# Expert weights of a mixture-of-experts layer loaded and multiplied in blocks of 1024 columns instead of 512

## What is computed

```python
def swiglu(x, w13, w2):
    gate, up = jnp.split(x @ w13, 2, axis=-1)
    return (jax.nn.silu(gate) * up) @ w2

def moe_swiglu(x, router, w13, w2):
    ...
    for e in range(N_EXPERTS):
        out = out + gates[..., e:e + 1].astype(x.dtype) * swiglu(x, w13[e], w2[e])
    return out
```

## Time and profile before

| | |
|---|---|
| median of 3 runs | 1877.17 us (1876.15 to 1878.55) |
| the profiled execution | 1874.99 us, its span 1873.2 us |
| matmuls busy (PE) | 1777.7 us, 95% |
| VectorE busy | 1303.8 us, 70% |
| ScalarE busy | 979.8 us, 52% |
| HBM read | 464.36 MB, 248 GB/s over the span |

### The profile page before, as it was taken

One profiled execution on the slowest core, in us unless ns is written; L12 is line 12 of the kernel. 1 busy time (PEld: TensorE's weight loads), 2 busy tenths in 40 slices (PEclk: granted clock), 3 DMA queues, 4 the chain that ended last, 5 costly groups with the idle time before them and its releaser, 6 DMA issues.

```text
span 1873.2 us, 21553 instructions
## 1 busy us (share of the span) xinstructions
PE 1777.7 (95%) x7962; PEld 1390.5 (74%) x7962; DVE 1303.8 (70%) x1217; ACT 979.8 (52%) x861; POOL 13.8 (1%) x22
## 2 busy tenths in 40 slices
PE   7999998999989998888999999999999999999996
PEld 6846674788867465747788888888888888888885
DVE  5464544445454554445988989889899898898996
ACT  4333122344233331314767767777677777776773
POOL 0000000000000000000000000000000000000000
PEclk9998799999999988997999999999999999999998
DMA  8523052454545231346999999999999999999991
GB/s 288 180 90 112 22 181 90 164 184 170 178 160 180 90 112 61 120 143 233 349 366 347 367 342 364 369 347 361 345 360 371 344 360 359 355 364 342 365 359 63
DMA packets 206471, 466.19 MB, mean 249 GB/s; under 512 B 11952, under 2 KB 14416, under 8 KB 206416
## 3 DMA queue, kind: packets, MB, share of 16 engines
q1 hardware_dynamic: 200880, 463.76, 68.9%
q10 hardware_dynamic: 5536, 1.68, 0.4%
HBM read 464.36 MB, written 1.05 MB: 248 GB/s over the span
## 4 chain that ended last, share of the span: by engine, by line
PE 90%; DVE 6%; ACT 2%; issue 1%; DMA 1%; POOL 0%; ACTq 0%; DVEq 0%; SPq 0%
PE ps L1427 22%; PE ps L1823 16%; PE ps L1825 16%; PE ps L1824 16%; PE ps L1454 6%; PE ps L1745 3%; PE ps L1803 2%; PE ps L1812 1%; PE ps L1618 1%; DVE w_lo L871 1%; PE ps L1388 1%; PE ps L1671 1%; PE ps L1653 1%; PE ps L1537 1%; PE ps L1580 1%
## 5 line engine op out<-in xcount | busy, mean ns | idle before, releaser
L871 DVE TENSOR_TENSOR w_lo<-ring,w_hi 128x2048 fp32r<-128x2048 f32 x336 | 767.7, 2289 | 120.5 <-ACT w_hi L556 117.5
L556 ACT CAST w_hi<-ring 128x2048 fp32r<-128x2048 f32 x336 | 641.9, 1911 | 280.1 <-PE ps L1825 265.1
L1823 PE MATMUL ps<-w_hi,xe_hi 128*128 128x512 f32 x896 | 353.2, 394 | 3.2 <-DVE w_lo L871 1.8
L1825 PE MATMUL ps<-w_hi,xe_lo 128*128 128x512 f32 x896 | 349.3, 390 | 0.0
L1824 PE MATMUL ps<-w_lo,xe_hi 128*128 128x512 f32 x896 | 348.7, 389 | 0.0
L1823 PEld LDWEIGHTS ps<-w_hi,xe_hi 128*128 128x128 f32 x896 | 168.2, 188 | 38.7 <-DVE w_lo L871 2.7
L1825 PEld LDWEIGHTS ps<-w_hi,xe_lo 128*128 128x128 f32 x896 | 168.1, 188 | 35.8
L1824 PEld LDWEIGHTS ps<-w_lo,xe_hi 128*128 128x128 f32 x896 | 168.4, 188 | 33.8
L1823 PE MATMUL ps<-w_hi,he_hi 128*128 128x512 f32 x448 | 178.2, 398 | 0.0
L1825 PE MATMUL ps<-w_hi,he_lo 128*128 128x512 f32 x448 | 174.8, 390 | 0.0
L1824 PE MATMUL ps<-w_lo,he_hi 128*128 128x512 f32 x448 | 174.4, 389 | 0.0
(11 more groups left out here) (260 smaller groups left out, 1846.1 us busy)
## 6 DMA issues: line engine op xcount, KB each, us to landing
ring<-in_moe_w_dram SPq DMA_DIRECT2D x336, 1024.0 KB, 5.5
ring<-in_ffd_w_dram SPq DMA_DIRECT2D x31, 1024.0 KB, 5.0
ring<-in_w_in_dram SPq DMA_DIRECT2D x24, 1024.0 KB, 5.5
ring<-in_xa_wkv_dram SPq DMA_DIRECT2D x16, 1024.0 KB, 5.0
ring<-in_w_out_dram SPq DMA_DIRECT2D x8, 1024.0 KB, 5.0
ring<-in_xa_wq_dram SPq DMA_DIRECT2D x8, 1024.0 KB, 4.9
ring<-in_xa_wo_dram SPq DMA_DIRECT2D x8, 1024.0 KB, 5.1
ring<-in_ffd_w_dram SPq DMA_DIRECT2D x4, 512.0 KB, 3.6
```

The lines of the kernel that those rows point to most:

```text
L556: act.copy(w_hi[:, q % SPLIT_SLOTS, :], ring[:, q % RAW_SLOTS, :]).then_inc(hi_ready, 1)
L871: dve.tensor_tensor(w_lo[:, q % SPLIT_SLOTS, :], ring[:, q % RAW_SLOTS, :], w_hi[:, q % SPLIT_SLOTS, :].bitcast(F32), ALU.subtract).then_i ...
L1823: pe.matmul(ps[:, bank, :], x_hi, hi[:, c, cols], start=first, stop=False)
L1825: return pe.matmul(ps[:, bank, :], x_lo, hi[:, c, cols], start=False, stop=last)
```

## The change

Gate and up are taken in blocks of 1024 columns: three wide blocks m = 0, 1, 2 and one of 512 columns (m = 3). A half of a wide block is 2 chunks of 128 rows times 1024 columns (still 1 MB, runs of 4 KB), and a wide block has four halves of gate (q = 8m to 8m + 3), then four of up (8m + 4 to 8m + 7). The last block keeps halves of 4 chunks times 512 columns, two of gate (24, 25), two of up (26, 27). Gate uses banks 0 and 1, up banks 2 and 3, for every block. The silu reads two banks in one operation, behind high(6), (14), (22) and, one bank, (28). The hge operations come in pairs behind low(10), (18), (26), and one behind (30). The transposes stand behind halves 11, 13, 19, 21, 27, 29, 31, and he_hi and he_lo four halves later. TensorE waits for the silu before each gate block and for the hge before each up block. In a wide half each row chunk is multiplied into one bank and then the other, three matmuls each. Nothing else moves; the scatter is that of the kernel before.

```diff
--- before.py
+++ after.py
@@ -75,10 +75,27 @@
 HIGH_SLOTS = 4
 MOE_PAIRS = F_MOE // N
 ITEM_HALVES = 6 * MOE_PAIRS
+WIDE = F_MOE // (2 * N)
+BLOCKS = WIDE + 1
+
+
+def moe_half(q):
+
+    if q < 8 * WIDE:
+        return q // 4 % 2, 2 * (q % 4), 2, q // 8 * 2 * N, 2 * N
+    r = q - 8 * WIDE
+    return r // 2, 4 * (r % 2), 4, WIDE * 2 * N, N
+
+
+GATE_DONE = [8 * m + 4 for m in range(WIDE)] + [4 * MOE_PAIRS - 2]
+UP_DONE = [8 * m + 8 for m in range(WIDE)] + [4 * MOE_PAIRS]
+SILU_AT = [q + 2 for q in GATE_DONE]
+HIDDEN_AT = [q + 2 for q in UP_DONE]
 UNITS = 7
 
 
-TURNED_AT = [4 * n + 11 for n in range(MOE_PAIRS - 1)] + [35]
+TURN_AT = [11, 13, 19, 21, 27, 29, 31]
+TURNED_AT = [q + 4 for q in TURN_AT]
 GATHERED_AT = [37, 40]
 SCATTERED_AT = [4, 5, 10, 11]
 ADDED_AT = [7, 8, 13, 14]
@@ -365,7 +382,7 @@
 
         def half_view(buffer, q, slots):
 
-            return buffer[:, q % slots, :].rearrange("p (c n) -> p c n", c=4 if q < 4 * MOE_PAIRS else 2)
+            return buffer[:, q % slots, :].rearrange("p (c n) -> p c n", c=moe_half(q)[2] if q < 4 * MOE_PAIRS else 2)
 
         def piece_bank(i):
 
@@ -436,9 +453,9 @@
             def item_half(q, i, e):
 
                 if q < 4 * MOE_PAIRS:
-                    c0 = (q // 2 % 2) * F_MOE + q // 4 * N
-                    r = 4 * (q % 2)
-                    src = a["moe_w13"][0, e].rearrange("(c p) n -> p c n", p=P)[:, r:r + 4, c0:c0 + N]
+                    g, r, chunks, c0, width = moe_half(q)
+                    c0 += g * F_MOE
+                    src = a["moe_w13"][0, e].rearrange("(c p) n -> p c n", p=P)[:, r:r + chunks, c0:c0 + width]
                 else:
                     r = 2 * (q - 4 * MOE_PAIRS)
                     src = a["moe_w2"][0, e].rearrange("(c p) n -> p c n", p=P)[:, r:r + 2, :]
@@ -754,12 +771,12 @@
 
                     if q == SPLIT_SLOTS - 1:
                         take_y(i - 1)
-                    if q % 4 == 0 and 4 <= q <= 4 * MOE_PAIRS:
-                        n = q // 4 - 1
-                        act.wait_ge(half_used, ITEM_HALVES * i + (4 * n + 2 + SPLIT_SLOTS))
-                        if n >= 2:
-                            act.wait_ge(he_ready, MOE_PAIRS * i + n)
-                        act.activation(sge[:, n % 2, :], ps[:, 2 * (n % 2), :], ACT.Silu).then_inc(g_taken, 1)
+                    if q in SILU_AT:
+                        m = SILU_AT.index(q)
+                        banks = 2 if m < WIDE else 1
+                        act.wait_ge(half_used, ITEM_HALVES * i + (GATE_DONE[m] + SPLIT_SLOTS))
+                        act.wait_ge(he_ready, MOE_PAIRS * i + (2 * m + 1))
+                        act.activation(sge[:, 0:banks, :], ps[:, 0:banks, :], ACT.Silu).then_inc(g_taken, 1)
                     if q in TURNED_AT:
                         n = TURNED_AT.index(q)
                         misc(n, i, he_hi[:, 4 * n:4 * n + 4, :], 4, he_split)
@@ -1338,14 +1355,15 @@
                         take_y(i - 1)
                     if not first and q in ADDED_AT:
                         add_up(i - 1, ADDED_AT.index(q))
-                    if q % 4 == 2 and 6 <= q <= 4 * MOE_PAIRS + 2:
-                        n = (q - 6) // 4
-                        dve.wait_ge(g_taken, MOE_PAIRS * i + (n + 2))
-                        dve.wait_ge(half_used, ITEM_HALVES * i + (4 * n + 4 + SPLIT_SLOTS))
-                        if n >= 2:
-                            dve.wait_ge(misc_ready[n % 2], 5 * i + (n // 2 + 1))
-                        dve.tensor_tensor(hge[:, n % 2, :], sge[:, n % 2, :], ps[:, 2 * (n % 2) + 1, :], ALU.mult)\
-                            .then_inc(he_ready, 1)
+                    if q in HIDDEN_AT:
+                        m = HIDDEN_AT.index(q)
+                        dve.wait_ge(g_taken, BLOCKS * i + (m + 2))
+                        dve.wait_ge(half_used, ITEM_HALVES * i + (UP_DONE[m] + SPLIT_SLOTS))
+                        for n in range(2 * m, min(2 * m + 2, MOE_PAIRS)):
+                            if n >= 2:
+                                dve.wait_ge(misc_ready[n % 2], 5 * i + (n // 2 + 1))
+                            dve.tensor_tensor(hge[:, n % 2, :], sge[:, n % 2, :], ps[:, 2 + n % 2, :], ALU.mult)\
+                                .then_inc(he_ready, 1)
                     if q == 20:
                         select(i + 1)
                         for t in range(T):
@@ -1843,22 +1861,24 @@
                     for b in range(2):
                         pe.wait_ge(misc_taken[b], 1)
                 for q in range(4 * MOE_PAIRS):
-                    n, g, r = q // 4, q // 2 % 2, q % 2
-                    taken = (g_taken, he_ready)[g]
+                    g, k0, chunks, _, width = moe_half(q)
+                    m = q // 8
                     pe.wait_ge(lo_ready, ITEM_HALVES * i + (q + 1))
-                    if r == 0 and n >= 2:
-                        pe.wait_ge(taken, MOE_PAIRS * i + n)
-                    elif r == 0 and n == 0:
-                        pe.wait_ge(taken, MOE_PAIRS * i + 1)
-                    for c in range(4):
-                        k = 4 * r + c
-                        ins = product(q, 2 * (n % 2) + g, xe_hi[:, k, :], xe_lo[:, k, :], c, slice(0, N),
-                                      k == 0, k == KC - 1)
+                    if k0 == 0 and g == 0:
+                        pe.wait_ge(g_taken, BLOCKS * i + (m + 1))
+                    elif k0 == 0:
+                        pe.wait_ge(he_ready, MOE_PAIRS * i + (2 * m + 1))
+                    for c in range(chunks):
+                        k = k0 + c
+                        for col in range(width // N):
+                            ins = product(q, 2 * g + col, xe_hi[:, k, :], xe_lo[:, k, :], c,
+                                          slice(col * N, (col + 1) * N), k == 0, k == KC - 1)
                     ins.then_inc(half_used, 1)
                     if q in SCATTERED_AT and not first:
                         scatter(i - 1, SCATTERED_AT.index(q))
-                    if q % 4 == 3 and n >= 1:
-                        turn_item(n - 1, i, n - 1)
+                    if q in TURN_AT:
+                        n = TURN_AT.index(q)
+                        turn_item(n, i, n)
                 for q in range(4 * MOE_PAIRS, ITEM_HALVES):
                     jj, r = divmod(q - 4 * MOE_PAIRS, 2)
                     pe.wait_ge(lo_ready, ITEM_HALVES * i + (q + 1))
@@ -1875,8 +1895,9 @@
                             ins = product(q, 4 + g, he_hi[:, k, :], he_lo[:, k, :], c, slice(g * N, (g + 1) * N),
                                           k == 0, k == 4 * MOE_PAIRS - 1)
                     ins.then_inc(half_used, 1)
-                    if q == 31:
-                        turn_item(6, i, 6)
+                    if q in TURN_AT:
+                        n = TURN_AT.index(q)
+                        turn_item(n, i, n)
                     if q == 33:
                         gather(i, 7, 0, i + 2)
                     if q == 37:
```

## The result

The median of 15 runs is **1880.38 us** (1878.21 to 1883.39) against 1877.19 us (1875.08 to 1879.29, 15 runs) for the kernel before: ratio **1.0018**, 95% interval 1.0010 to 1.0025, 3.2 us more. The profiled execution took 1882.28 us, its span is 1880.5 us.

The account below looks back on a forecast made before the run. TensorE was taken to bound the kernel, with loads hidden behind it. Profiled 1874.99 us + 1.4 (first item) + 0.6 (steady items) = 1877.0, which puts the median at 1879.2 us; range 1875.8 to 1885.0.

Parts of the forecast that it names:

- The sum: Profiled execution 1874.99 us + 1.4 (first item) + 0.6 (slack in steady items) = 1877.0; median from 1877.17 to 1879.2.
- Bound and loads: Expert part: TensorE sets the pace, so gate and up packets going from 2 to 4 KB gain nothing.
- The sign named for the landings: Loads of w13: packets halved in number, landing near 4.9 us, if the prediction was right.
- The first item: First of eight expert items: late ScalarE and VectorE work costs +0.45, +0.1, 0 and +0.85, together +1.4 us.
- Half 19: First item: VectorE lateness 2.21 us, less 0.75 paid = 1.46, cost 0.71 us.
- Steady items, halves 19 and 27: Behind the hge pairs lateness is 0.79 against 1.0 us of slack: 0.04 us a place, 15 places.
- The slow rival: Halves 19 and 27: hge pair takes 1.5 instead of 1.2 us, 15 places cost 5.1 us, 1883.7; chance 0.27.
- Part 3: Waits that move: gate blocks on silu and up blocks on hge are met; no cost counted.
- 0.6 for the slack: Steady items: 0.04 us a place at halves 19 and 27, 15 places, 0.6 us in all.
- the turn behind q = 31: It needs he_lo 4, now at VectorE's 31 instead of 27; 2.4 us of slack claimed.
- steady items at 123.3 to 123.5 us: Sign that the prediction is right: time of one expert item after the first.
- a steady item of 123.8 us or more with gaps at halves 19 and 27: Sign that the prediction is wrong: bunched VectorE work crosses the slack in every item.

Follow-up runs that it names:

- runs 3: Changed kernel, each half of the expert weights loaded by two transfers: all packets 2 KB, 1881.05 us; control keeping 4 KB, 1881.63 us.
- run 4: Changed kernel, expert-weight halves in two transfers, each issued four halves later: 2004.18 us with 4 KB packets, 2027.99 us with 2 KB.
- run 1: Changed kernel, but TensorE waits for one hge of block 2 instead of both before the last up block: 1877.72 us, ratio 0.9998.
- run 5: Kernel of run 1, selection operations moved from behind low(20) to behind low(18): two moved, 1878.98 us; all four, 1883.42 us.
- run 2: Changed kernel with the hge pair of block 2 on VectorE behind low(27) instead of low(26): 1912.47 us, ratio 1.0186.

## Why the prediction was right, and where it was not

The time was: 1879.2 predicted, 1880.4 measured; no difference over 0.2% forecast and 0.18% found, on the slower side as forecast. The sum was +2.0 us, +3.2 was measured, inside the +0.5 to +3.7 given. That it came this close is in part luck: the largest term of the measured difference stood at nothing in the sum.

**Bound and loads: right.** TensorE sets the pace, the loads follow; runs 3 and 4 show both halves of that, no effect as the kernel stands and 24 us where loads bind. The pitch of the matmuls did not move with packets or banks: a half of a wide block without a loss still takes 2.72 us (893.04 - 890.32 between two starts of high in the first item). The sign named for the landings, near 4.9 us for w13, did not come; at 6.7 us they still fit into the lead of 14.7. The silu of two banks took 1.02 us where I took 1.03 (line, group, busy and mean ns):

```profile
L779 ACT ACTIVATE sge<-ps 128x1024 f32<-128x1024 f32 x24 | 24.5, 1023 | 0.0
```

**The first item: right in mechanism, one term off and one missing.** ScalarE's starts of high show when TensorE finished a half (high(q) starts when half q - 3 ends). The rows for all halves of the table but 12, and at the end VectorE's low(19):

```profile
886.94 1.91 ACT L573 CAST w_hi<-ring 128x2048 fp32r<-128x2048 f32 x1 [0.31 <-PE ps L1843]
890.32 1.92 ACT L573 CAST w_hi<-ring 128x2048 fp32r<-128x2048 f32 x1 [1.46 <-PE ps L1843]
...
913.85 1.91 ACT L573 CAST w_hi<-ring 128x2048 fp32r<-128x2048 f32 x1 [0.33 <-PE ps L1843]
...
917.26 1.91 ACT L573 CAST w_hi<-ring 128x2048 fp32r<-128x2048 f32 x1 [1.51 <-PE ps L1843]
...
922.70 1.91 ACT L573 CAST w_hi<-ring 128x2048 fp32r<-128x2048 f32 x1 [0.80 <-PE ps L1843]
925.66 1.91 ACT L573 CAST w_hi<-ring 128x2048 fp32r<-128x2048 f32 x1 [1.06 <-PE ps L1843]
...
929.70 1.92 ACT L573 CAST w_hi<-ring 128x2048 fp32r<-128x2048 f32 x1 [1.20 <-PE ps L1843]
...
932.70 1.91 ACT L573 CAST w_hi<-ring 128x2048 fp32r<-128x2048 f32 x1 [0.62 <-PE ps L1843]
...
920.19 2.28 DVE L888 TENSOR_TENSOR w_lo<-ring,w_hi 128x2048 fp32r<-128x2048 f32 x1
```

| half | predicted cost | measured: start to start, less 2.72 (and 0.44 with transposes) |
|---|---|---|
| 7 | 0.69 | 890.32 - 886.94 - 2.72 = 0.66 |
| 12 | 0.82 | 905.20 - 901.22 - 3.16 = 0.82 |
| 16 | 0.75 | 917.26 - 913.85 - 2.72 = 0.69 |
| 19 | 0.71 | 925.66 - 922.70 - 2.72 = 0.24 |
| 20 | 0.88 | 929.70 - 925.66 - 3.16 = 0.88 |
| 21 | as before | 932.70 - 929.70 - 2.72 = 0.28 |

Half 19 was over by 0.47. The step that failed is "1.93 - 0.51 + 0.61 - 0.51 + 1.20 - 0.51 = 2.21 for half 19": I let lateness drain by 0.51 a half everywhere. The four transposes behind half 13 also make TensorE 0.44 us later, so high(17) may start 0.44 later without loss, and that much lateness is gone by half 19: 1.46 - 0.44 = 1.02, close to the 1.0 of slack. The trace shows it: high(19) ends at 917.26 + 1.91 = 919.17, low(19) starts at 920.19, some 0.98 late, and half 19 cost 0.24. I had used the transposes as slack for the next three halves and not as drain for the ones behind. The total of the first item came out at 1.5 against 1.4 predicted only because half 26 added some 0.5 there (101.62 - 101.10, run 1), which is luck.

**Steady items, halves 19 and 27: right.** 0.04 us a place, 0.08 an item, was predicted from a lateness of 0.79; 0.77 was measured, and with the wait at half 26 shortened, items are 0.03 us longer than before (run 1). The slow rival, that the pair of hge takes 1.5 us, did not happen: in the first item low(19) follows the start of the pair, 919.00, after 1.19 us. Run 5 shows that it would have cost what was said: 0.4 us more work there costs 0.29 us an item.

**Part 3: wrong, and it holds most of the measured difference.** The step that failed is "up block m for the hge pair m - 1 (VectorE, 8m + 2, against TensorE's 8m + 4): met." That is true for m = 1 and 2. The last block has only two gate halves, so its up block starts at half 26, not at 28, and the pair that it waits for stands behind low(26) on VectorE. There low ends about 1.0 us ahead of the half by the earlier trace rows, and the pair needs 1.20: a wait by the numbers of the prediction itself. It costs 0.43 in each of the seven steady items and 0.52 in the first, 3.55 us between the profiles of the changed kernel and of run 1, where the sum had 0 for it and 0.6 for the slack. The prediction's 1.4 for the first item stands against 0.98 in run 1, its 0.6 for the slack against 0.12. Before the change, the block of 512 had no such meeting: its up halves waited for the hge of two blocks earlier.

Beside it, two slips of no weight: by its own terms the turn behind q = 31 has 3.0 us of slack and not 2.4, and the upper end of the range is 1885.2.

The range held the time since it took in a cost of the slow rival's kind, 15 places of 0.34; the true one had 8 places of about 0.45 and another cause. Of the signs listed, "steady items at 123.3 to 123.5 us" did not come, and "a steady item of 123.8 us or more with gaps at halves 19 and 27" came nearest, 123.76, with its gap at half 26.

## What to carry to other kernels

When a rule for a schedule (8m + 2 against 8m + 4) is checked, check the odd block at the end with its own numbers: there the distances are shorter than in the formula. Here bigger packets paid only where an engine waited for a load; the DMA share of 0.98 didn't show that, the list of waits did. And a wait before writing a set of banks can be given bank by bank: here one count less gave back some 3 us.

## What the runs showed of the hardware

- A gap of 2.8 to 2.95 us without a matmul was followed by a lower granted clock in seven of eight items (run 2): behind the one at 1202.21, matmuls stood 0.43 us apart (1.2 GHz) for the first seven, then 0.23 again (2.4 GHz). In the eighth the clock stayed at 1.00 behind a gap of 2.81. After the gaps of 0.17 us in the changed kernel it stayed at 1.00. The wait grew by 2.64 us and cost 2.64 where the clock stayed, up to 4.31 where it fell.
- An operation that lands just before TensorE needs it isn't free: with low(19) 0.17 and 0.56 us later than the slack of 1.0 allows, the item lost 0.12 to 0.18 us more than that (run 5). In the changed kernel the first matmul behind the gap at half 26 is 0.33 us from the next instead of 0.227, which is 0.1 of it.
- The DMA share is no measure of reserve: at 0.97 to 0.99 the loads had some 8 us of slack (14.7 us of lead, median landings of 5 to 7), and at 0.91 they bound the kernel (run 4).
